# Attention units handled by repetition, and the output stored by tiles: one step of a hybrid decoder on one core

## The reference, cut to what matters

```
def masked_softmax(s, mask):
    s = jnp.where(mask, s, NEG_INF)
    m = jnp.max(s, axis=-1, keepdims=True)
    e = jnp.where(mask, jnp.exp(s - m), 0.0)
    return e / jnp.maximum(jnp.sum(e, axis=-1, keepdims=True), 1e-30)
```

```
h = layer_norm(ALPHA * h + f, ln_fg, ln_fb)
return h + jax.nn.sigmoid(h @ w_gate) * (p @ w_proj)
```

## Time and profile before

| quantity | us |
|---|---|
| median of 3 runs (1639.3 to 1641.22) | 1640.69 |
| the profiled execution | 1640.43 |
| its span | 1638.8 |
| TensorE busy, 12538 matmuls and 12538 weight loads | 1579.2 (96% of the span) |
| VectorE busy | 1000.2 (61%) |
| ScalarE busy | 722.3 (44%) |
| POOL busy | 322.6 (20%) |

### The profile page before, as it was taken

One profiled execution on the slowest core, in us unless ns is written; L12 is line 12 of the kernel. 1 busy time (PEld: TensorE's weight loads), 2 busy tenths in 40 slices (PEclk: granted clock), 3 DMA queues, 4 the chain that ended last, 5 costly groups with the idle time before them and its releaser, 6 DMA issues.

```text
span 1638.8 us, 31404 instructions
## 1 busy us (share of the span) xinstructions
PE 1579.2 (96%) x12538; PEld 1541.5 (94%) x12538; DVE 1000.2 (61%) x1576; ACT 722.3 (44%) x1316; POOL 322.6 (20%) x742
## 2 busy tenths in 40 slices
PE   8999899988999999999999999999999999999995
PEld 8999777868999999999999998999999999999995
DVE  3346687775787345535567786868863554355582
ACT  4445677863444334313435437634542342234250
POOL 4711344520054012102200000002620220122000
PEclk9999999999999999999999999999999999999998
DMA  7645000043122322222221322231322222222221
GB/s 267 140 113 208 1 1 1 17 169 113 66 89 82 101 78 91 91 79 89 91 102 65 100 82 72 94 121 52 103 83 98 78 91 91 87 83 101 91 74 59
DMA packets 41483, 148.00 MB, mean 90 GB/s; under 512 B 6305, under 2 KB 8369, under 8 KB 40897
## 3 DMA queue, kind: packets, MB, share of 16 engines
q1 hardware_dynamic: 35568, 123.35, 23.2%
q0 software_dynamic: 5776, 22.71, 4.0%
HBM read 140.57 MB, written 9.10 MB: 91 GB/s over the span
## 4 chain that ended last, share of the span: by engine, by line
PE 87%; DVE 6%; ACT 3%; issue 2%; DMA 0%; POOL 0%; ACTq 0%; DVEq 0%
PE PS L2025 75%; PE PS L2187 2%; PE PS L2149 2%; PE PS L2063 2%; PE PS L2064 2%; ACT ARENA L836 1%; PE PS L2320 1%; DVE SMALL L1348 1%; PE PS L2139 1%; PE PS L2140 1%; DVE LO L472 1%; DVE X L1641 1%; PE PS L2173 1%; ACT HI L466 0%; DVE ARENA L1724 0%
## 5 line engine op out<-in xcount | busy, mean ns | idle before, releaser
L2025 PE MATMUL PS<-XH,HI 128*128 128x272 f32 (+1 forms) x1936 | 405.7, 291 | 10.4 <-DVE XL L1192 8.5
L2025 PE MATMUL PS<-XH,LO 128*128 128x272 f32 (+1 forms) x1936 | 401.4, 289 | 0.0
L2025 PE MATMUL PS<-XL,HI 128*128 128x272 f32 (+1 forms) x1936 | 400.4, 288 | 0.0
L466 ACT ACTIVATE HI<-RAW 128x1024 fp32r<-128x1024 f32 x223 | 235.2, 1057 | 256.5 <-PE PS L2025 232.4
L472 DVE TENSOR_TENSOR LO<-RAW,HI 128x1024 fp32r<-128x1024 f32 x223 | 274.1, 1230 | 106.4 <-ACT HI L466 106.1
L2025 PE MATMUL PS<-GH,HI 128*128 128x272 f32 (+1 forms) x1504 | 315.6, 291 | 5.5 <-ACT ARENA L1113 3.5
L2025 PEld LDWEIGHTS PS<-XH,HI 128*128 128x128 f32 x1936 | 306.4, 189 | 12.3 <-DVE LO L472 8.5
L2025 PE MATMUL PS<-GH,LO 128*128 128x272 f32 (+1 forms) x1504 | 311.4, 289 | 0.0
L2025 PE MATMUL PS<-GL,HI 128*128 128x272 f32 (+1 forms) x1504 | 311.0, 288 | 0.0
L2025 PEld LDWEIGHTS PS<-XL,HI 128*128 128x128 f32 x1936 | 304.9, 188 | 0.1
L2025 PEld LDWEIGHTS PS<-XH,LO 128*128 128x128 f32 x1936 | 303.7, 188 | 0.0
(11 more groups left out here) (375 smaller groups left out, 1906.2 us busy)
## 6 DMA issues: line engine op xcount, KB each, us to landing
RAW<-in_w_stream SPq DMA_DIRECT2D x223, 512.0 KB, 3.3
ARENA<-in_cache_cmp POOLq DMA_DIRECT2D x32, 128.0 KB, 3.1
out_win_old<-in_win_copy POOLq DMA_DIRECT2D x1, 4064.0 KB, 18.3
X<-in_x SPq DMA_DIRECT2D x4, 544.0 KB, 7.4
X<-in_x POOLq DMA_DIRECT2D x1, 2176.0 KB, 8.2
out_y<-X POOLq DMA_DIRECT2D x1, 2176.0 KB, 6.9
ARENA<-in_cache_sel POOLq DMA_DIRECT2D x16, 128.0 KB, 2.5
ARENA<-in_cache_win POOLq DMA_DIRECT2D x4, 512.0 KB, 4.8
```

Of the source, the lines that this page charges most:

```text
L466: nc.scalar.activation(HI[:, s * CH:(s + 1) * CH], RAW[:, (c % RAWS) * CH:(c % RAWS + 1) * CH], ACT.Copy).then_inc(hi_ready, 1)
L2025: ins = mm(PS[0:rows, b + h, 0:width], w[:, 0:rows], cols(part, h), start=first and len(parts) == 2 and n == 0, stop=last and len(parts) == 1)
```

## The change

1. **Parts.** The semaphores of the attention count parts: a narrow unit is one part, a wide unit two, one for each repetition. `FIRST_PART`, `part` and `shares_free` give the counts, and all waits on these semaphores, SP's too, are rewritten to them.
2. **Wide units by repetition.** A wide unit has two maxima, two reciprocals, and signals after each repetition of the scores, exponentials and reciprocals; POOL waits for each repetition by itself. When unit u is wide as well, ScalarE's order becomes copy of repetition 0 (of u), exponentials of repetition 0 (of u + 2), copy of 1, exponentials of 1; VectorE's becomes both maxima (u + 2), low part 0 (u), reciprocal 0 (u + 2), low part 1, reciprocal 1. When unit u is narrow, the parts follow its single block.
3. **The last tile by halves.** TensorE computes tile 7 of the last gate for the first 272 tokens over all eight k, then for the other 272; sigmoid, product and sum follow in two halves with semaphores of their own (`last_half`, `last_gate`, `y_half`).
4. **The output by tiles.** The single transfer from POOL's queue goes. SP issues, after its last weight load, one transfer of 272 KB for each of the tiles 0 to 6 when it is ready, then two of 136 KB for the halves of tile 7, and waits for all nine.

```
+        FIRST_PART = [0]
+        for u in range(64):
+            FIRST_PART.append(FIRST_PART[-1] + (1 if narrow(u) else 2))
+        FIRST_PART += [FIRST_PART[64] + v for v in range(1, 5)]
+        def parts_of(u):
+            return (None,) if narrow(u) else (0, 1)
+        def part(u, r):
+            return FIRST_PART[u] + (2 if r == 1 else 1)
+        def shares_free(u, r):
+            return FIRST_BLOCK[u] + (1 if narrow(u) or r == 0 else 2)
...
@@ SyncE @@
-                    sp.wait_ge(s_done, 56)
+                    sp.wait_ge(s_done, FIRST_PART[56])
...
+            def store(c0, c1):
+                sp.dma_start(outs["y"][:, c0:c1], X[:, c0:c1]).then_inc(y_out, 16)
+            for k in range(KT - 1):
+                sp.wait_ge(y_ready, KT + k + 1)
+                store(k * TOK, (k + 1) * TOK)
+            sp.wait_ge(y_half, 1)
+            store((KT - 1) * TOK, (KT - 1) * TOK + HALF)
+            sp.wait_ge(y_ready, 2 * KT)
+            store((KT - 1) * TOK + HALF, KT * TOK)
+            sp.wait_ge(y_out, 16 * (KT + 1))
@@ POOL @@
-                pool.wait_ge(c_ready, u + 1)
                 for r in range(2):
+                    pool.wait_ge(c_ready, part(u, None if narrow(u) else r))
...
-            pool.wait_ge(y_ready, 16)
-            pool.dma_start(outs["y"], X[:, :]).then_inc(out_dma, 16)
-            pool.wait_ge(out_dma, 96)
+            pool.wait_ge(out_dma, 80)
@@ ScalarE @@
-                act.wait_ge(negmax_ready, u + 1)
+                act.wait_ge(negmax_ready, part(u, part_r))
                 if u >= 2:
-                    act.wait_ge(pt_done, blocks_done(u - 2))
+                    act.wait_ge(pt_done, shares_free(u - 2, part_r))
...
+                due = list(parts_of(u + 2)) if u < 62 else []
                 for m, r in blocks_of(u):
                     act.wait_ge(pt_done, m + 1)
                     s.activation(side_by_side(PTSH[n % 2], u, r), ...).then_inc(pt_act, 1)
+                    if r == 0 and due == [0, 1]:
+                        exps(u + 2, due.pop(0))
...
-                if u < 62:
-                    exps(u + 2)
+                for r in due:
+                    exps(u + 2, r)
...
+                    if layer == 1 and k == 7:
+                        act.wait_ge(y_ready, 14)
+                        act.wait_ge(last_half, 1)
+                        s.activation(LT[:, TOK:TOK + HALF], banks(o)[:, 0, :], ACT.Sigmoid).then_inc(last_gate, 1)
+                        act.wait_ge(tile_done, o + 1)
+                        s.activation(LT[:, TOK + HALF:2 * TOK], banks(o)[:, 1, :], ACT.Sigmoid).then_inc(act_took, 1)
+                        continue
@@ VectorE @@
+            def neg_max(u, r):
+                dve.wait_ge(s_done, part(u, r))
+                v.tensor_reduce(of_part(16, u, r), scores_of(u, r), AX_X, ALU.max, negate=True).then_inc(negmax_ready, 1)
+            def one_over_sum(u, r):
+                dve.wait_ge(p_ready, part(u, r))
+                v.reciprocal(of_part(160, u, r), of_part(64, u, r)).then_inc(c_ready, 1)
...
+                due = list(parts_of(u + 2)) if u < 62 else []
+                for r in due:
+                    neg_max(u + 2, r)
                 for m, r in blocks_of(u):
                     dve.wait_ge(pt_act, m + 1)
                     sub_lo(side_by_side(PTSL[n % 2], u, r), ...)
+                    if r == 0 and due == [0, 1]:
+                        one_over_sum(u + 2, due.pop(0))
...
+                for r in due:
+                    one_over_sum(u + 2, r)
@@ TensorE @@
                 for r in (slice(0, 2),) if narrow(u) else (0, 1):
+                    if u >= 2:
+                        pe.wait_ge(p_ready, FIRST_PART[u - 1] if narrow(u) or r or narrow(u - 2) else part(u - 2, r))
...
-                    ins = mm(at[:, r, w - P:w], DIAG[:, :], mask, start=False, stop=True)
-                ins.then_inc(s_done, 1)
+                    mm(at[:, r, w - P:w], DIAG[:, :], mask, start=False, stop=True).then_inc(s_done, 1)
...
-                for n in range(3, 8):
+                for n in range(3, 8 - layer):
                     tile(go + n, gc + n, range(KT), bh3, bl3, 0)
+                if layer == 1:
+                    ready(go + 7, gc + 7)
+                    for h, done in enumerate((last_half, tile_done)):
+                        for k in range(KT):
+                            products(go + 7, gc + 7, k, bh3, bl3, k, k == 0, k == 7, hs=(h,), done=done)
```

More of the change, by code:

```diff
@@ L824, in _, with exps @@
             P4 = PB.rearrange("p (u r k) -> p u r k", u=2, r=2)
-            def exps(u):
+            def exps(u, part_r):
                 w = P * (unit(u)[0] + 1)
-                act.wait_ge(negmax_ready, u + 1)
+                act.wait_ge(negmax_ready, part(u, part_r))
                 if u >= 2:
-                    act.wait_ge(pt_done, blocks_done(u - 2))
+                    act.wait_ge(pt_done, shares_free(u - 2, part_r))
                 elif u == 1:
                     act.wait_ge(gate_dma, 16 * 34)
-                for r in range(2):
+                for r in (0, 1) if part_r is None else (part_r,):
                     c = 2 * (u % 2) + r
@@ L837, in exps @@
                                        bias=SMALL[:, 16 + c:17 + c], accum_out=SMALL[:, 64 + c:65 + c])
-                    if r == 0:
+                    if part_r is None and r == 0:
                         chain.did(ins)
@@ L855, in _ @@
             cmp_exp(0)
-            exps(0)
-            exps(1)
+            exps(0, None)
+            exps(1, None)
             compressed_values()
@@ L1416, in out_lo @@
                 sub_lo(heads_of(XL3, n), sums_of(n), heads_of(XH3, n), ot_lo)
-            neg_max(0)
-            neg_max(1)
+            neg_max(0, None)
+            neg_max(1, None)
             chain.sync()
@@ L1423, in _ @@
             largest(1)
-            one_over_sum(0)
+            one_over_sum(0, None)
             below_largest(1)
-            one_over_sum(1)
+            one_over_sum(1, None)
             compressed_values()
@@ L1839, in tail @@
                     lt = LT[:, (k % 2) * TOK:(k % 2 + 1) * TOK]
+                    if layer == 1 and k == 7:
+                        for h, (gate, at, done) in enumerate(((last_gate, 1, y_half), (act_took, taken(o)[1], y_ready))):
+                            dve.wait_ge(gate, at)
+                            chain.did(v.tensor_tensor(half(PP3[:, k, :], h), half(PP3[:, k, :], h), half(lt, h), ALU.mult))
+                            chain.sync()
+                            v.scalar_tensor_tensor(out=half(X3[:, k, :], h), in0=half(X3[:, k, :], h),
+                                                   scalar=par(f"ln_fb{layer}", k), in1=half(PP3[:, k, :], h),
+                                                   op0=ALU.add, op1=ALU.add).then_inc(done, 1)
+                        continue
                     dve.wait_ge(act_took, taken(o)[1])
@@ L2016, in ready, with products @@
                     wait_taken(pe, PAIR_BEFORE[o], t)
-            def products(o, c, k, xh, xl, x, first, last, rows=P, width=HALF):
+            def products(o, c, k, xh, xl, x, first, last, rows=P, width=HALF, hs=(0, 1), done=tile_done):
                 cols = lambda t, h: t[:, x, h, :] if width > HALF else t[:, x, h * HALF:(h + 1) * HALF]
@@ L2023, in products @@
                     for n, part in enumerate(parts):
-                        for h in range(2):
+                        for h in hs:
                             ins = mm(PS[0:rows, b + h, 0:width], w[:, 0:rows], cols(part, h),
@@ L2027, in products @@
                 if last:
-                    ins.then_inc(tile_done, 1)
+                    ins.then_inc(done, 1)
             def tile(o, c, ks, xh, xl, x0, rows=P, t=None, each=None, width=HALF):
@@ L2224, in sample_trans @@
                 u = 64 + x
-                pe.wait_ge(p_ready, u + 1)
+                pe.wait_ge(p_ready, FIRST_PART[u] + 1)
                 pe.wait_ge(pt_act, transposed(u))
@@ L2300, in _ @@
                 values(15, quarter)
-            pe.wait_ge(negmax_ready, 66)
+            pe.wait_ge(negmax_ready, FIRST_PART[66])
             pe.wait_ge(ot_lo, 15)
```

33 lines of the change are left out of this document (11 added, 22 removed).

## The result

| | before | with the change |
|---|---|---|
| median, same chip | 1640.88 us (4 runs) | 1621.37 us (4 runs, 1619.51 to 1621.75) |
| ratio | | 0.9881, 95% interval 0.9864 to 0.9898 |
| profiled execution | 1640.43 us | 1621.75 us |
| span | 1638.8 us | 1620.1 us |

What follows compares the result with a forecast made beforehand. TensorE was taken as the bound, so gains come only where it stands still or at the end. 1640.43 - 5.9 (end) - 2.8 (attention) = 1631.7; with the median 0.26 above, 1632.0 us, range 1628 to 1636.5.

Steps and rivals of the forecast that it cites:

- The step that failed: End of program: 9.5 us between the store's landing and the span's end taken as fixed, untouched by the change.
- rival 3: End: small store slower, or the 9.5 us hang on more; half the gain, 3 us, lost; 1635.0 us; 8 in 100.
- The rest of the end: Last matmul to last landing: shorter sigmoid, product and sum and smaller last store, 9.42 to 3.53 us, gaining 5.9.
- u = 4 to 7: Attention, narrow units ahead of wide: head start shortens the compressed block's wait, clock still down; gain 0.9 us.
- u = 12 to 15: Attention: wide units follow at once and repetition 1's transposes wait behind copy 1; gain only 0.1 us.
- u = 20 to 23: Attention: TensorE's 1.67 us wait at 233.89 loses 1.1, part of it coming back; gain 0.75 us.
- u = 28 to 31: Attention: 0.9 us off the transposes' wait at 259.90 plus half of the clock's fall, some 0.6; gain 1.5 us.
- the 384-column groups and the last one: Attention: low part 1 later in three full groups, -1.0 us; last group's wait for POOL goes, gain 0.6.
- The ring: Wide unit behind wide: cycle of maximum, exponentials and now copy 1, period 2.89 us against 2.80; no gain.
- Rival 1: Attention gives nothing, 0 to 1.5 us of head starts lost; 1635.1 us; 20 in 100.
- Rival 2: Attention: both falls of the clock (187 to 197, 255 to 264) go, 6.5 us in all; 1628.3 us; 12 in 100.
- Rival 4: Attention: VectorE's queue limits wide units, 0.3 us each, 9.6 in 32; slower, 1644.4 us; 3 in 100.

Runs made afterwards that it cites:

- experiment 4: The changed kernel with one more instruction on POOL, its last: a wait for the last sum over y that moves no data; 1627.42 us.
- experiment 6: The changed kernel with tile 6 of y stored by POOL, SP waiting for it and POOL issuing nothing behind; 1624.67 us.
- sp_whole: The kernel before with its single 2176 KB store of y issued and awaited by SP in place of POOL; 1630.5 us.
- experiment 10: The whole change, but with the old order of ScalarE and VectorE between two wide units; 1619.88 us.
- experiment 9: The kernel before with parts 1 and 2 of the change, but the old order of ScalarE and VectorE between two wide units; 1636.26 us.
- experiment 1: The kernel before with each half of the change alone: parts 1 and 2 (attention) 1636.83 us, parts 3 and 4 (tail) 1625.28 us.
- experiment 7: The changed kernel with tile 7 whole: no halves in its matmuls, sigmoid, product, sum or store; 1622.28 us.
- experiment 8: The kernel before with parts 1 and 2 in the 512-column units only, 1635.43 us, or in the 384-column units only, 1639.16 us.
- tail_only: The kernel before with parts 3 and 4 of the change alone, the attention left as it was; 1625.28 us.

## Why the prediction was wrong

**The step that failed** is the one I wrote in a sentence: "Behind it the span has 1638.8 - 1629.3 = 9.5 us left ... I take both as they are: they belong to the end of any program here, and the change touches nothing in them." The row stood in front of me: the last engine with an instruction was POOL. I asked what the transfer costs and not whose end the 9.5 us were. They are POOL's: the span ends 9.6 us behind the end of its last wait with no transfer at all (experiment 4), 9.4 behind a small issue (6), and 0.4 behind the last landing when SP is last (2). The change takes POOL's last wait from 1629.3 back to its other stores, of which it issues the last at 1503.65, so its stopping lies under the matmuls. In the sum this term stood at nothing; it was 9.1 us (9.5 before, 0.4 after), of the 10.6 by which the forecast missed. I even had the place in rival 3, but on the wrong side: "the 9.5 us behind the landing hang on more than the landing" was weighed only as a way to gain less.

**The rest of the end held.** 5.9 us were predicted for the shorter chain and the smaller last store. From the start of the last sigmoid to the last landing 1629.30 - 1619.90 = 9.40 us became 1619.72 - 1616.58 = 3.14, so it was 6.3. With the 9.1 that is the 15.4 of the tail. (The ladder's 3.4 + 2.3 = 5.7 leaves out 0.6 that came with the move to SP: a transfer of 6.6 instead of 6.9 us, and an issue 0.3 us sooner behind the sum.) The three operations took 0.40, 0.44 and 0.50 us, exactly as interpolated. The store took 1.7 us and not 2.05. By the Trainium skill (DMA: Bandwidth & Descriptors, section Anatomy of one DMA — SWDGE (gpsimd) path) it would have been 2.3, an estimate from that page; that page's fit is for POOL's path, and here the transfer is SP's, so the row at 1.7 is no contradiction. The same fit gives 7.1 us for the old store of 2176 x 1024 bytes, where I wrote 7.0; nothing hangs on it. Nor did the cutting cost anything at the end: of nine transfers only the last shows, though the seven of 272 KB took 4.5 us each in the median.

**The attention held in sum, partly by luck.** Predicted 2.85, traced 3.3, measured alone 3.8 (2.3 to 5.2). By the copies of sums:

- u = 4 to 7: predicted 0.9. The lead at copy 0 is 1.16 us, but copy 0 starts anywhere from 194.45 to 197.71 in five executions with the old attention, so this term is not resolved.
- u = 12 to 15: predicted 0.1; +0.83 and -0.82 in the two steps, 0.01. Right: the head start is there and is lost again in the next step.
- u = 20 to 23: predicted 0.75; 1.32 - 0.09 = 1.23. The wait of 1.67 us ahead of the transposes became 0.58. The term was too small by 0.5.
- u = 28 to 31: predicted 1.5 with half of the clock's fall; 1.32 - 0.39 = 0.93 with the clock still at 0.81. The term was too large by 0.6, and its place was wrong too: the 1.57 us that were to shrink by 0.9 became 1.29, and the gain came from the wait of 1.30 us, of which 0.22 and 0.28 are left.
- the 384-column groups and the last one: predicted -1.0 and 0.6. The steps from copy 6 to 12 differ by 0.02 us and those from 12 to 15 by 0.03, both lost. Neither term is there: what a narrow step gains (up to 0.5 us) the wide one behind it loses.

Behind copy 0 the terms add up to 1.95 and the copies show 2.12, but only because errors of +0.5, -0.6, +1.0 and -0.6 cancel. The waits of TensorE that answer to the earlier trace rows, in the changed kernel:

```profile
231.61 1.33 PE L2200 MATMUL PS<-IDENT,ARENA 128*128 128x128 f32 x8 [0.58 <-DVE PTSL L1230]
...
256.43 1.08 PE L2208 MATMUL PS<-IDENT,SC 128*128 128x128 f32 x4 [1.29 <-DVE PTSL L1230]
...
338.02 0.52 PE L2200 MATMUL PS<-IDENT,ARENA 128*128 128x128 f32 x3 [0.33 <-DVE PTSL L1230]
338.76 0.52 PE L2200 MATMUL PS<-IDENT,ARENA 128*128 128x128 f32 x3 [0.23 <-POOL ARENA L658]
...
340.55 0.52 PE L2200 MATMUL PS<-IDENT,ARENA 128*128 128x128 f32 x3 [0.23 <-DVE PTSL L1230]
```

The 1.67 us went to 0.58, the compressed block's 1.57 only to 1.29, and POOL's 0.59 in the last group is replaced by three waits, 0.33 and 0.23 for low parts and 0.23 for POOL, 0.79 in all. What was late next was not TensorE, as I had said, but VectorE's low parts.

**The ring.** I forecast 2.89 us for a wide unit behind a wide one and called a period outside 2.7 to 2.9 a sign that I was wrong. VectorE's maxima in one wide group of the changed kernel (the fourth row is already the next, narrow unit):

```profile
203.08 1.29 DVE L1390 TENSOR_REDUCE SMALL<-PS 128x1 f32<-128x512 f32 x2
...
206.70 1.27 DVE L1390 TENSOR_REDUCE SMALL<-PS 128x1 f32<-128x512 f32 x2
...
210.04 1.27 DVE L1390 TENSOR_REDUCE SMALL<-PS 128x1 f32<-128x512 f32 x2
...
212.79 0.41 DVE L1390 TENSOR_REDUCE SMALL<-PS 128x2 f32<-128x256 f32 x1
```

The maxima of the kernel before that stand ahead of and behind the two in the earlier trace rows:

```profile
204.89 1.20 DVE L1348 TENSOR_REDUCE SMALL<-PS 128x2 f32<-128x1024 f32 x1
...
214.29 0.40 DVE L1348 TENSOR_REDUCE SMALL<-PS 128x2 f32<-128x256 f32 x1
```

The periods are 3.62, 3.34 and 2.75 us, against 3.80, 2.80 and 2.80 before. The 3.34 is outside, and so would the 3.80 before have been: the ring of 2.80 describes only two of the group's three periods. ScalarE's copy within the period of 3.34, at 207.50, waits 1.44 us for transposes of TensorE:

```profile
207.50 0.60 ACT L895 ACTIVATE PTSH<-PS 128x512 fp32r<-128x512 f32 x1 [1.44 <-PE PS L2200]
```

With a head start the chain seems to reach TensorE while this is still busy, and to give the time back: TensorE has products and scores in its queue ahead of these transposes, and its rows from 203.59 to their start at 206.87 show no wait. In the kernel of experiment 10 the periods are 3.62, 3.34 and 2.51. So part of the loss between wide units is the new order's, 0.21 of the 0.82 us lost in step 1 to 2 (experiment 9). The reason I gave (copy 1 enters the ring) fits that, but the reciprocal between the low parts was taken away with it. The rest of the loss is there in either order; that it is TensorE's own work is my reading of these rows, and no run tests it.

**The rivals.** Rival 1 (attention gives nothing) is refuted by experiment 1. Rival 2 (both falls of the clock go) did not happen in the profiled execution. The second fall was missing in those of experiments 4 and 7: granted 1.00 over 255 to 264, and step 5 to 6 took 13.26 and 13.25 us instead of 14.56. So the fall costs 1.3 us when it comes, in the same attention. But it is missing with the old attention too, in three of its five executions, and there step 5 to 6 takes 13.67 instead of 14.17 us. So no run shows that the change prevents it, and my half of a fall had no ground; what decides whether it comes is open. Compared without the fall on either side, the attention from the first to the last copy takes 159.1 to 159.2 us before and 156.4 with the change, 2.8 less; with the fall on both sides it is 159.6 to 159.8 and 157.6 to 157.8, 2.0 less. Rival 3 (the end does not follow) is refuted: the last store took 1.7 us, less than its neighbours. Rival 4: VectorE's busy time in the full stretch rose from 48.85 to 52.59 us and TensorE lost 0.5 there. The order that it blamed, reciprocal 0 ahead of low part 1, is among what experiment 9 puts back, and that is worth 1.35 us over all 32 wide units, not 9.6; the split as a whole costs 0.1 to 0.3 us in the 384-column units (experiment 8).

## What to carry to other kernels

Idle time behind the last landing is a term like any other: look which engine has the last instruction, and ask what the end would be if another had it. This kernel paid some 9 us for letting POOL wait for its own last store. Where a kernel ends the same way, let SP store and wait, and let POOL's last instruction, a bare wait included, end 10 us ahead of the rest, an estimate from the 9.4 to 9.6 us measured here (11.1 behind a store of 2176 KB). And when a chain is split to let its first half start early, keep the order of the work that was hidden under it: here the head start came from the split alone, and the interleaved order cost 1.35 us and brought nothing.

## What was not expected of the hardware

- From the last instruction of POOL to the end of the span: 9.5 us (before), 9.6 (a bare wait), 9.4 (a 272 KB issue), 11.1 (a 2176 KB issue that SP waits for). From the last landing on SP's queue: 0.4 us, in three kernels (`sp_whole`, `tail_only` and the change). What POOL does in that time the trace doesn't show. The other engines can't need nearly as long: in the change VectorE's last instruction ends at 1617.99 and ScalarE's at 1616.98, 2.1 and 3.1 us ahead of the end of the span.
- A store of 2176 KB takes 6.6 us from SP and 6.9 from POOL (6.8 to 7.3 in seven kernels); a store of 136 KB takes 1.7 us from SP. One of 272 KB takes 2.3 us from POOL (experiment 6) and 4.5 from SP, the median of six in the same execution.
- A fall of the clock from 2.4 to 1.2 GHz for part of 255 to 264 us (granted 0.81 or 1.00 over the stretch) comes in some executions of one kernel and not in others (step 5 to 6: 14.56 or 13.26 us with the change, 14.17 or 13.67 without).
